# Score matmuls of an attention stage on 32 or 64 contraction rows instead of 128 zero-padded ones, two maps issued in turn

## The reference, cut to what matters

```python
# A: 64 rows a head, keys of the own and the two previous chunks
s = jnp.einsum('bqkgd,bskd->bkgqs', qg, k).astype(jnp.float32) * HEAD_DIM ** -0.5
# B: two maps (m) a head, 32 rows each; w = p0 - lam * p1
s = jnp.einsum('bqhmd,bkhmd->bhmqk', q, k).astype(jnp.float32) * B_DIM ** -0.5
p = jax.nn.softmax(jnp.where(mask, s, NEG_INF), axis=-1)
w = p[:, :, 0] - lam * p[:, :, 1]
# C: 64 rows a head, plus differences of cumulative log forget gates
s = jnp.einsum('bqhd,bkhd->bhqk', q, k).astype(jnp.float32) * HEAD_DIM ** -0.5
```

## Time and profile before

| what | value |
|---|---|
| median of the two executions | 3518.47 us |
| span of the profiled execution (the page gives no separate time for it) | 3514.1 us |
| TensorE busy, weight loads busy | 3223.0 us, 2884.4 us |
| VectorE, ScalarE, GpSimd busy | 1718.7, 1076.7, 54.3 us |
| `attend`, layer 1 and 2 | about 411 to 825 us and 2124 to 2538 us of the span |

### The profile page before, as it was taken

How to read it: one execution, slowest core, us unless ns; L and a number is a source line. 1 busy time by engine, 2 the same in 40 slices (tenths; PEclk the granted TensorE clock), 3 DMA queues, 4 the chain that set the end, 5 groups by cost and what they waited for, 6 DMA issues and landing times. The chain is left out here.

```text
span 3514.1 us, 50348 instructions
## 1 busy us (share of the span) xinstructions
PE 3223.0 (92%) x18146; PEld 2884.4 (82%) x18146; DVE 1718.7 (49%) x4094; ACT 1076.7 (31%) x2321; POOL 54.3 (2%) x32
## 2 busy tenths in 40 slices
PE   0699899998899999999969997999898999999999
PEld 0589777786789999999958896777777999999998
DVE  0444378643244544545445445785434454454454
ACT  1332276553221111111123225665423111111111
POOL 0000010000000000000000001010000000000000
PEclk9899999998999999999989998999998999999999
DMA  7244544333021111111024445525132111111111
GB/s 170 79 138 133 161 122 106 88 82 116 18 66 36 41 49 36 53 37 36 24 92 124 132 136 138 131 69 137 35 94 59 44 36 54 36 36 54 36 36 60
DMA packets 368396, 274.96 MB, mean 78 GB/s; under 512 B 128546, under 2 KB 336366, under 8 KB 368186
## 3 DMA queue, kind: packets, MB, share of 16 engines
q1 hardware_dynamic: 368218, 272.70, 27.5%
HBM read 195.84 MB, written 78.62 MB: 78 GB/s over the span
## 5 line engine op out<-in xcount | busy, mean ns | idle before, releaser
L1515 DVE TENSOR_TENSOR x<-x,ffn_down 128x512 f32<-128x512 f32 x792 | 509.4, 683 | 0.0
L1537 DVE TENSOR_TENSOR ffn_xn<-ffn_xn,ffn_up 128x384 f32<-128x384 f32 x132 | 73.1, 554 | 758.1 <-ACT ffn_xn L1482 758.1
L418 PE MATMUL ffn_up<-ffn_h_hi,ffn_hi_g 128*128 128x384 f32 x1056 | 360.3, 341 | 15.2 <-DVE ffn_h_lo L243 10.5
L419 PE MATMUL ffn_up<-ffn_h_lo,ffn_hi_g 128*128 128x384 f32 x1056 | 359.7, 341 | 0.0
L420 PE MATMUL ffn_up<-ffn_h_hi,ffn_lo_g 128*128 128x384 f32 x1056 | 359.4, 340 | 0.0
L418 PE MATMUL ffn_up<-ffn_h_hi,ffn_hi_u 128*128 128x384 f32 x1056 | 355.2, 336 | 3.2 <-DVE ffn_lo_u L243 3.2
L420 PE MATMUL ffn_up<-ffn_h_hi,ffn_lo_u 128*128 128x384 f32 x1056 | 354.8, 336 | 0.0
L419 PE MATMUL ffn_up<-ffn_h_lo,ffn_hi_u 128*128 128x384 f32 x1056 | 354.8, 336 | 0.0
L991 PE MATMUL att_S<-att_kT,att_qT 128*128 128x512 f32 (+3 forms) x864 | 322.9, 490 | 33.1 <-DMA att_qT<-scratch_qkT 25.9
L1482 ACT ACTIVATE ffn_xn<-ffn_up 128x384 f32<-128x384 f32 x132 | 64.9, 491 | 861.1 <-PE ffn_up L420 861.1
L418 PE MATMUL prj_acc<-prj_w_hi,prj_h_hi 128*128 128x384 f32 (+2 forms) x864 | 318.8, 369 | 0.0
(11 more groups left out here) (173 smaller groups left out, 5352.5 us busy)
## 6 DMA issues: line engine op xcount, KB each, us to landing
ffn_raw_g<-in_w_gate SPq DMA_DIRECT2D x44, 512.0 KB, 4.0
ffn_raw_u<-in_w_up SPq DMA_DIRECT2D x44, 512.0 KB, 5.1
ffn_raw_d<-in_w_down SPq DMA_DIRECT2D x44, 512.0 KB, 5.1
scratch_qkv<-prj_nat SPq DMA_DIRECT2D x72, 192.0 KB, 1.9
prj_w_raw<-in_w_in SPq DMA_DIRECT2D x64, 192.0 KB, 2.6
scratch_qkv<-prj_nat SPq DMA_DIRECT2D x36, 256.0 KB, 2.1
att_kT<-scratch_qkT SPq DMA_DIRECT2D x16, 576.0 KB
att_vn<-scratch_qkv SPq DMA_DIRECT2D x16, 576.0 KB, 8.4
```

The lines of the kernel that those rows point to most:

```text
L418: pe.matmul(out, l_hi, r_hi, start=first, stop=False)
L419: pe.matmul(out, l_hi, r_lo, start=False, stop=False)
L1515: dve.tensor_tensor(x, x, down[:, (q * ND + n) % 4, :], ALU.add).then_inc(added, 1)
L1537: dve.tensor_tensor(a32[:, b, :], sg[:, b, :], up[:, b, 1, 0:384], ALU.mult).then_inc(gated, 1)
```

## The change

Queries are packed: `qT` has one slot a buffer, map m in its own rows. A score matmul names only the 32 (B) or 64 (A, C) rows of its map in `qT` and `kT`. GpSimd writes no zeros to `qT`, and SyncE no longer waits for it. The two jobs of a B unit are issued in turn, chunk by chunk, so a B unit now waits until both halves of `S` are free. In a sample unit the new keys' scores (now L994) come ahead of the cached keys' (L998); those keep 128 rows and the zeros in `qpast`.

```diff
-    qT = ph.sb("qT", [P, 2, 4, TOK])
+    qT = ph.sb("qT", [P, 2, TOK])
...
-                sp.wait_ge(q_zeroed[b], sum(x.index % 2 == b and fresh(x) for x in groups[:g.index + 1]))
                 for m in range(g.maps):
-                    sp.dma_start(qT[m * g.D:(m + 1) * g.D, b, m, :], t["qkT"][g.q_row(m):g.q_row(m) + g.D, :]).then_inc(sem, 16)
+                    sp.dma_start(qT[m * g.D:(m + 1) * g.D, b, :], t["qkT"][g.q_row(m):g.q_row(m) + g.D, :]).then_inc(sem, 16)
...
-            for b in range(2):
-                pool.memset(qT[:, b, 0:2, :], 0.0).then_inc(q_zeroed[b], 1)
...
-                if 1 <= g.index < NG - 1 and fresh(groups[g.index + 1]):
-                    pool.memset(qT[:, (g.index + 1) % 2, :, :], 0.0).then_inc(q_zeroed[(g.index + 1) % 2], 1)
...
+                first = jobs_to[u]
+                work = []
                 for r in range(g.per_head):
-                    job = jobs_to[u] + r
                     m = h * g.per_head + r
-                    if job >= 2:
-                        pe.wait_ge(biased, job - 1)
-                    out, q = S[:, job % 2, :], qT[:, b, m, i * P:(i + 1) * P]
...
+                    rows_ = slice(m * g.D, (m + 1) * g.D)
+                    work.append((first + r, m, rows_, S[:, (first + r) % 2, :], qT[rows_, b, i * P:(i + 1) * P]))
+                if jobs_to[u + 1] >= 3:
+                    pe.wait_ge(biased, jobs_to[u + 1] - 2)
+                if i < TP:
+                    k0, n = g.keys(i)[0] * P, g.n_cols(i)
+                    for c in range(0, n, 512):
+                        w = min(512, n - c)
+                        for job, m, rows_, out, q in work:
+                            last = pe.matmul(out[:, c:c + w], q, kT[rows_, b, k0 + c:k0 + c + w], start=True,
                                              stop=not (g.kind == "C" and c + w == n))
```

More of the change, by code:

```diff
@@ L833, in attend @@
     S, TR, O = ph.ps("S", [P, 2, SEQ]), ph.ps("TR", [P, 2, 512]), ph.ps("O", [P, 2, 512])
-    qk_in, v_in, q_zeroed = ([ph.sem(f"{n}{i}") for i in range(2)] for n in ("qk_in", "v_in", "q_zeroed"))
+    qk_in, v_in = ([ph.sem(f"{n}{i}") for i in range(2)] for n in ("qk_in", "v_in"))
     kp_in, vp_in, qpast_zeroed, qpast_in, const_in = (
@@ L864, in attend @@
     n_qk = {"A": 2 + 1 + 4, "B": 4 + 1 + 4, "C": 2 + 1 + 6}
-    def fresh(g):
-        return g.index < 2 or "B" in (g.kind, groups[g.index - 2].kind)
     def to(g, parity, count):
@@ L980, in score @@
                     pe.wait_ge(prepared, 1)
+                first = jobs_to[u]
+                work = []
                 for r in range(g.per_head):
-                    job = jobs_to[u] + r
                     m = h * g.per_head + r
-                    if job >= 2:
-                        pe.wait_ge(biased, job - 1)
-                    out, q = S[:, job % 2, :], qT[:, b, m, i * P:(i + 1) * P]
[L987 to L991, removed]
-                                             stop=not (g.kind == "C" and c + w == n))
-                        if g.kind == "C":
-                            last = pe.matmul(out[:, n - P:n], ident_b[:], mask_b[:], start=False, stop=True)
-                    else:
+                    rows_ = slice(m * g.D, (m + 1) * g.D)
+                    work.append((first + r, m, rows_, S[:, (first + r) % 2, :], qT[rows_, b, i * P:(i + 1) * P]))
@@ new lines, in score @@
+                if jobs_to[u + 1] >= 3:
[6 more added lines that the diff above has]
+                            last = pe.matmul(out[:, c:c + w], q, kT[rows_, b, k0 + c:k0 + c + w], start=True,
+                                             stop=not (g.kind == "C" and c + w == n))
+                            if c + w == n and g.kind != "C":
+                                last.then_inc(scored, 1)
+                    if g.kind == "C":
+                        for job, m, rows_, out, q in work:
+                            pe.matmul(out[:, n - P:n], ident_b[:], mask_b[:], start=False, stop=True).then_inc(scored, 1)
+                else:
+                    for job, m, rows_, out, q in work:
+                        pe.matmul(out[:, g.n_past:g.n_samp], q, kT[rows_, b, SEQ:TOK], start=True, stop=True, skip_group_check=True)
+                    for job, m, rows_, out, q in work:
@@ L996, in score @@
                         for c in range(g.nb):
                             x = m * g.nb + c
[L998 to L1001, removed]
+                            last = pe.matmul(out[:, 0:g.n_past], qpast[:, x, :], kpT[:, x * g.n_past:(x + 1) * g.n_past],
+                                             start=(c == 0), stop=(c == g.nb - 1))
```

## The result

The kernel after takes 3739.14 us (median of two executions, 3738.51 and 3739.76) against 3518.47: ratio 1.0629, 95% interval 1.0598 to 1.066. It is slower by 6%, and the forecast of 3540 us with its range to 3585 was wrong.

A forecast was written before the change was run, and what follows sets the result against it. TensorE, busy 92% of the span, was taken to bound the kernel. Terms +41 (A and C), 0 (B) and -20 (no zeros) sum to +21 on 3514.1 us: 3535 for the span, 3540 us for the median, range 3505 to 3585.

The forecast's parts named there:

- no zeros to write: GpSimd's memset of `qT` holds up VectorE's L1212, for which TensorE waits; without it -20 us (15 to 20).
- tiles in A and C, clock held: A and C in two layers: 356 changes of array shape at 0.115 us each, +41 us (32 to 53).
- B, clock held: B: overlap of two maps against waits for both halves of `S` and changes of shape, net 0 us (-22 to +17).
- gaps in B or A: Rival: gaps bring the granted clock down, one group in three at 0.9, about 15 us a layer, 3570 us; chance 0.04.
- Fewer rows alone saves nothing: Score matmuls: columns set a pass's time and a map's columns stay, so fewer rows save nothing.
- Change of array shape: 64- or 32-row scores between 128-row transposes and values: entering and leaving cost 0.23 us, 0.115 a change.
- the order of issue brings the overlap: B: issued in turn, map 0's second pass runs beside map 1's first; eight passes take five pass times.
- Memset: GpSimd's `qT` memset delays L1212, chiefly in A's third group (8.2 and 6.8 us) and B's first (2.3 a layer).
- Loads: Same bytes in the same DMAs; only a layer's first group could start earlier; 0 taken, -4 us as the end.
- The mark I had set for being wrong: Forecast wrong if A and C scores follow at 0.11 us, or a unit's two 256-column passes exceed 0.5 us.
- The rival of the loads: Second weight load can't run under a pass on the same rows: 0.11 us each, +72 us, 3612 us; chance 0.08.

The follow-up runs named there:

- all_filled: fill_rows with, in B too, the other head's two maps as an unused pair beside each first chunk; 3578.78 us, ratio 1.0189.
- late_zeros: Kernel before, with GpSimd's memset of `qT` put off until VectorE has scaled the sample units of the groups before; 3491.16 us, ratio 0.9938.
- full_rows: Kernel after with every score matmul of `qT` on all 128 rows, packing, loads, order and waits kept; 3519.1 us, ratio 1.0022.
- shape_only: full_rows plus one 64-row matmul of 16 columns ahead of each unit's scores; 3634.84 us, ratio 1.0348.
- fill_rows: Kernel after plus, in A and C, an unused matmul on the other 64 rows beside each unit's first chunk; 3598.43 us, ratio 1.0247.
- same_rows: fill_rows with the unused extra matmul on the map's own 64 rows instead of the other 64; 3863.99 us (one execution).
- b_filled: Kernel after with A and C on zero-padded 128 rows, and B's first chunks beside an unused pair of the other head's maps; 3522.07 us, ratio 1.0022.
- b_apart: Kernel after with A and C on zero-padded 128 rows, B's maps issued one after the other, each awaiting its half of `S`; 3564.14 us, ratio 1.0152.

## Why the prediction was wrong

The sum of the two `attend` stages, by the lengths of the groups in the traces, is this; "held" means with the clock held by the fills of all_filled, and late_zeros is its base:

| step | forecast | measured |
|---|---|---|
| no zeros to write | -20 | -20.6 (late_zeros against before) |
| tiles in A and C, clock held | +41 (32 to 53) | +52.5, the fill included |
| B, clock held | 0 | +0.2 in the one group that ran all at full clock |
| clock in A and C | 0 | +138.8 (after against all_filled) |
| clock in B | 0 | +49 (after against late_zeros, so with the row above in it) |
| sum | +21 | +219.9 |

**The step that failed** is the clock. It stood among the rivals with a chance of 0.04 and 30 us, as "gaps in B or A" that bring it down, priced as one group in three at 0.9. Measured it is about 188 us (138.8 + 49; the 49 includes whatever B's second group would cost at full clock, where no run had it). The mechanism was wrong, not only the size: full_rows and shape_only show that it is not gaps, fill_rows and same_rows that it is the rows left idle, in B by b_filled in part. The error began with the sentence "Fewer rows alone saves nothing": I asked what fewer rows save and not what they cost. The trace of before could not answer that: it has one 64-row transpose in each sample unit, which gave the price of a change of shape, and six passes on 32 rows at the program's start, which ran at 1.2 GHz behind a wait and so say nothing of a full clock. With an unknown of this kind the range should have carried the full price of the other clock level: TensorE busy for some 383 us a layer in `attend` at 2.4 GHz would take twice that at 1.2. The top of the range, 3585 us, was 12 above what its named terms add to (3518.5 + 53 - 15 + 17 = 3573.5).

**Change of array shape.** Right. A's third group, at full clock and without fill, has TensorE busy for 29.09 us against the 25.12 of the earlier trace rows: 3.97 us, 18 units of 0.22, forecast 0.23; in length it is 3.2 us (29.19 against 25.95 in late_zeros). C pays more in all_filled, 6.5 us in its second group (61.44 against 54.97). Part of that is the fill and its wait: in the kernel after, at full clock and without fill, a C unit of seven key tiles takes 3.25 us from its scores to the next unit's (795.34 to 798.59), before the change 3.01 (751.43 to 754.44), 0.24 more, and 18 units of that are 4.3 us.

**B.** The net of zero held in the first group, by parts that were both mis-sized (the second never ran all at full clock): the overlap is full, four pass times for eight, and VectorE takes the gain back (its 54.75 us busy and the waits for L1177, 0.90 us at 558.64 where I had 0.4 to 0.7; in all_filled's full-clock group they come to 7.5 us, in late_zeros' to none). That the order of issue brings the overlap was wrong, by b_apart. Without overlap the wait for both halves costs 5.0 us in B's first group of layer 1 (full_rows against late_zeros).

**Memset.** Right, in size and place. **Loads.** Right that they run ahead. The mark I had set for being wrong, over 0.5 us for a unit's two passes of 256 columns, was badly set: from their start to the transposes it is 0.63 us (517.59 to 518.22), before 0.49, and the 0.14 more is the change of shape, which the mark left out. The rival of the loads would have put 0.11 a unit on top of the 0.23; measured is 0.22 in all.

**Still open.** What decides at which level a stretch of 64-row passes runs. In the kernel after the first group of A is at 0.50 and the third at 1.00 in both layers, with the same kind of units. The clock comes back at about 495 us in layer 1, in the second group, and at about 2342 in layer 2, at that group's end; in same_rows it comes back in layer 2's first group, at about 2345. Each time a sample unit's work on 128 rows (scores of cached keys, transposes of weights) had just run, but the sample units before had brought nothing (0.50 over the whole first group in the kernel after). In C's second group the first head stays at 1.00 and the second falls. Why the fill holds B in part only is open too. No run here took the history of a group apart.

## What to carry to other kernels

Before naming fewer rows in a matmul, ask what works on the other rows at the same time: here row tiles kept the clock best where they filled the 128 rows together, and a busy TensorE on a half-used array could lose half its clock, for the passes on 128 rows around it too. Even with the clock held, the tiles gained no time in this kernel. A change on the bounding engine whose clock behaviour the trace does not show needs the other clock level in its range. When a removal is worth something for a reason beside the point (here the memset that held VectorE up), take that part alone: one wait gave 0.6%, the rest of the change cost 7% (1.0629 / 0.9938).

## What the runs showed of the hardware

- Stretches with score passes on 64 rows and TensorE busy nearly all the time were granted 1.2 GHz (0.50 over 45.02 us in A, busy 44.67). With the other 64 rows filled, C's groups stayed at 2.4 GHz (1.00 over 61.45 us) and A's came up to it (1.00 over 29.29 us, its second group).
- Where the clock was up, 64-row passes of 256 columns also ran at 2.4 GHz (1.00 over 29.19 us, and over 35.49 us with such passes doubled on the same rows).
- A matmul on 64 free rows beside one on the other 64 cost A next to nothing: 29.29 us a group with fill, 29.19 without, both at full clock.
- Matmuls on separate rows ran side by side in full, also when a whole map with two chunks was issued ahead of the other: both maps in 2.87 us, where the columns of one alone come to 2.56 at the pace worked out above.
- An added pair of changes of shape with a 16-column matmul between them costs 0.34 us a unit (98.5 us over 288 units, by the profiled spans).
